# Last block: the convolution's taps over eight steps instead of seven, its norm, gates and output product one step later

## The chip, the cores and the metric

The kernel runs as one program on one of the eight cores of a Trainium2 chip. The metric is the device time of one launch in microseconds (us). Three runs of the kernel before gave a median of 1036.96 us (1036.89 to 1037.16). The profile shown here is one further execution that took 1037.11 us. A core has a matrix engine (PE, TensorE, with its weight loads listed apart as PEld), a vector engine (DVE), an activation engine (ACT), a general engine (POOL) and a queue that issues DMAs (SP). Each works through its own list of instructions in order, and they wait for each other by semaphores.

## The reference, cut to what matters

The program computes a chain of blocks on 256 tokens of 1024 channels: a gated linear attention with a feed-forward net, an attention with a feed-forward net, and then the last block, in which alone the change lies. Its input `h` goes through one wide matrix, whose columns are cut into parts:

```python
c_val, c_gate, c_og, ts, r_og, g_conv, g_rwkv = jnp.split(p, SPLITS, axis=-1)   # p = h @ w_in
u = c_val * sigmoid(c_gate)
u = causal_depthwise_conv(u, conv_k) + conv_b         # 31 taps for each of 1024 channels
u = layernorm(u, ln_g, ln_b)                          # over the channels
y_conv = (silu(u) * silu(c_og)) @ w_conv_out
y_rwkv = rwkv7_branch(ts, r_og) @ w_rwkv_out          # 16 heads of 64, a recurrence over the tokens
m = sigmoid(g_conv) * y_conv + sigmoid(g_rwkv) * y_rwkv
x = x + gate * (m @ w_out)                            # then a last rmsnorm
```

The two branches depend on `h` alone and meet in `m`.

## The kernel before

Activations lie transposed, channels on the 128 partitions and tokens along the free axis; 1024 channels are eight tiles of 128 x 256. Every product with a weight matrix is cut into dense blocks of 256 output columns. For a block, SP loads 1 MB of weights into one of three `raw` buffers; ACT copies it into a rounded high part (line 296, two halves), DVE subtracts to get the low part (line 304, two halves), and PE sums three products for each of eight input tiles and two output halves: high by high, high by low, low by high (lines 318 to 320), 48 matmuls in all. The blocks use the buffers in turn, so the split of block n + 3 waits until block n is done.

The last block has 48 dense blocks: r, k, v (inputs of the recurrence), val and gate (the convolution's input), og (the convolution's output gate), rog (the recurrence's), gr and gc (the two sigmoid gates of `m`), cout (the product with `w_conv_out`), rout (with `w_rwkv_out`) and out (with `w_out`), four of each. The recurrence works on pairs of heads, eight in all, as a software pipeline of steps s = -2 to 8 (loops over s and r at lines 1358 of PE, 1970 of ACT and 2748 of DVE). In step s, `chain` runs the recurrence over four chunks of tokens for pair s, `middle` prepares pair s + 1 (scores, then an inverse of a triangular matrix built up in five levels that go PE, DVE, PE, ACT and round again), `front` prepares pair s + 2, and `gn` normalises pair s - 1. A step has 12 slots (r = 0 to 11); each slot has two half slots (q = 0 to 23). These parts leave short stretches on every engine, and a table `STEP_BLOCKS` puts dense blocks between them: `put_blocks` cuts each block into eight units of six matmuls and deals them evenly over the 24 half slots of the step, together with the halves of the split of the block two further on ("hi" for ACT, "lo" for DVE), the evacuation from PSUM by ACT ("take", at the block's last unit) and what DVE does with it ("use", one half slot later). The order of `STEP_BLOCKS` is also the order of the loads on SP. All of this is fixed when the program is written: there is no scheduler.

The convolution is 248 instructions of DVE (31 taps for eight tiles, line 2614, the first of a tile line 2610), dealt over half slots by `TAP_SLOTS`: 164 half slots, from q = 4 of step -1 to the end of step 5. Three pairs of tiles are summed (`three_pairs`) when their taps are done. Then comes its layer norm, `ln`, in step 6: PE sums over channels (line 1087), DVE subtracts the mean (line 2632, eight tiles), ACT squares (line 1849), DVE folds (lines 2637, 2638), PE sums (line 1092), ACT takes the logarithm and the exponential (lines 1431, 1432), DVE scales (line 2643, eight tiles), ACT applies silu (line 1858, eight tiles). Each og block is evacuated by ACT into a gate tile (line 1817), DVE multiplies (line 2586), ACT rounds the product (`conv_y_hi`, line 1872) and DVE takes the low part (line 2656). These four pieces are the input of the cout blocks, whose units wait for them one by one (semaphore `conv_y_split`).

Before, og0 to og3 stand in step 6 behind the norm, and step 7 has gc3 first and then cout0 to cout3. In step 8, which has no recurrence left but the normalisation of the last pair, the first two rout blocks run tile by tile (`rout_part`) in banks 4 and 5 as the tiles of the recurrence's output come. The rest of rout and out stands behind the loop. The line numbers below are those of the kernel before; PE's small matmuls named there are line 1225 (first product of a chunk in `chain`), 1246 (`u_product`, which needs ACT's copy of line 1958), 1148 (scores), 1171 (`seeds`, which needs three results of DVE's `middle` at r = 0), 1195 and 1198 (the inverse's steps).

Of the kernel before, what the change touches and what calls it, by code (L numbers as in the profile page):

```python
# [184 lines left out]
def program(nc, a, out):  # L185
    with ExitStack() as ctx:
# [389 lines left out]
        for q, item in enumerate((("hi", N_ROUT + 2, 0), ("hi", N_ROUT + 2, 1), ("lo", N_ROUT + 2, 0),  # L576
                                  ("lo", N_ROUT + 2, 1))):
            put_at(8, 1 + q, item)
        for g in range(14):
            put_at(8, 12 * g // 14, ("rout_part", g // 7, g % 7))  # L580
# [13 lines left out]
        def _(pe):  # L594
# [455 lines left out]
            def unit(n, u):  # L1050
# [9 lines left out]
                if u == 7:  # L1060
                    last.then_inc(block_done, 1)

            def rout_part(j, k):

                n = N_ROUT + j
                if k == 0:
                    pe.wait_ge(w_lo_ready, n + 1)
                    bank_freed(n)
                pe.wait_ge(sem("rwkv_split"), k + 1)
                for m in range(2):  # L1070
                    ps, wh, wl, xh, xl = operands(n, m, k)
# [1798 lines left out]
```

## Time and profile before

| what | value |
|---|---|
| median of three runs | 1036.96 us |
| the profiled execution | 1037.11 us, its span 1035.3 us |
| PE busy, share of the span | 1006.3 us, 97% |
| PEld busy | 930.6 us, 90% |
| DVE busy | 869.3 us, 84% |
| ACT busy | 608.7 us, 59% |
| granted clock of PE in the steps of the last block | 1.00 |

The last block takes the part of the span from about 603 us on. A step is read best by PE's own marks: the matmuls of `u_product` at r = 1 (line 1246) of steps 0 to 7 start at 681.96, 720.18, 758.82, 798.53, 836.45, 870.28, 902.82 and 947.30 us, so that the distance of two of them is one step, from slot 1 to slot 1. A busy share in these stretches counts instructions that run; the waits are a view of their own, and where a matmul waits it is PEld that stands, since the weight load comes first.

### The profile page before, as it was taken

What the parts mean: (1) busy time and instruction counts of PE and PEld (TensorE: products, weight loads), DVE (VectorE), ACT (ScalarE), POOL (GpSimd) and SP (SyncE); (2) the same over time, 40 slices, a digit from 0 to 9 for tenths busy, and PEclk for the clock granted to TensorE, in tenths of its full rate; (3) what the DMA queues carried; (4) which work ended last, traced back from release to release, by engine and by line L of the source; (5) the groups of instructions that cost most, each with busy time, mean ns of one, the idle gap of its engine ahead of it and who ended that gap; (6) DMA issues with size and microseconds to landing.
All of it is one profiled execution on the core that took longest, in us unless ns stands there. A gap on an engine that the chain in (4) does not pass through costs nothing.

```text
span 1035.3 us, 23881 instructions
## 1 busy us (share of the span) xinstructions
PE 1006.3 (97%) x10130; PEld 930.6 (90%) x10130; DVE 869.3 (84%) x1447; ACT 608.7 (59%) x878; POOL 18.3 (2%) x38
## 2 busy tenths in 40 slices
PE   7999999999999999999999999999999999999997
PEld 6999999999999989989898998889998988889996
DVE  7866699899989886999899897998998999965474
ACT  7755664444446756554444577656667667686443
POOL 2000000000000000000000000000000000000000
PEclk9999999999999999999999999999999999999998
DMA  9662457777654515576765646333323322234531
GB/s 279 217 200 93 156 186 251 233 243 226 200 174 151 164 45 183 200 231 226 250 224 184 203 132 195 115 93 122 125 90 117 121 87 83 84 124 152 175 123 41
DMA packets 136071, 168.20 MB, mean 162 GB/s; under 512 B 3216, under 2 KB 125328, under 8 KB 135728
## 3 DMA queue, kind: packets, MB, share of 16 engines
q1 hardware_dynamic: 132080, 153.44, 46.0%
q0 software_dynamic: 3904, 13.50, 4.1%
q8 instruction: 66, 1.08, 0.4%
q14 instruction: 21, 0.17, 0.0%
HBM read 164.83 MB, written 2.10 MB: 161 GB/s over the span
## 4 chain that ended last, share of the span: by engine, by line
PE 73%; DVE 18%; ACT 5%; issue 2%; DMA 2%; SPq 0%; DVEq 0%; ACTq 0%
PE banks L353 13%; PE banks L318 9%; PE banks L319 8%; PE banks L320 8%; PE banks L355 7%; DVE hf L2614 3%; DVE w_parts L280 3%; DVE w_parts L304 2%; PE banks L655 2%; PE bank L657 2%; PE bank L655 2%; PE bank L659 2%; PE banks L657 2%; PE banks L659 2%; ACT w_parts L275 1%
## 5 line engine op out<-in xcount | busy, mean ns | idle before, releaser
L280 DVE TENSOR_TENSOR w_parts<-raw,w_parts 128x2048 fp32r<-128x2048 f32 x95 | 217.1, 2288 | 27.2 <-ACT w_parts L275 26.8
L353 PE MATMUL banks<-x_parts,w_parts 128*128 128x512 f32 x640 | 227.1, 399 | 0.0
L318 PE MATMUL banks<-x_parts,w_parts 128*128 128x256 f32 x704 | 211.7, 301 | 0.0
L319 PE MATMUL banks<-x_parts,w_parts 128*128 128x256 f32 x736 | 207.8, 282 | 0.0
L320 PE MATMUL banks<-x_parts,w_parts 128*128 128x256 f32 x704 | 198.7, 282 | 0.0
L275 ACT ACTIVATE w_parts<-raw 128x2048 fp32r<-128x2048 f32 x95 | 180.9, 1905 | 3.6 <-PE banks L810 2.1
L355 PE MATMUL banks<-x_parts,w_parts 128*128 128x256 f32 x640 | 179.8, 281 | 0.0
L353 PEld LDWEIGHTS banks<-x_parts,w_parts 128*128 128x128 f32 x640 | 120.3, 188 | 29.0
L318 PEld LDWEIGHTS banks<-x_parts,w_parts 128*128 128x128 f32 x704 | 134.0, 190 | 9.5 <-issue 3.3
L319 PEld LDWEIGHTS banks<-x_parts,w_parts 128*128 128x128 f32 x736 | 140.7, 191 | 0.6 <-issue 0.5
L320 PEld LDWEIGHTS banks<-x_parts,w_parts 128*128 128x128 f32 x704 | 134.3, 191 | 0.0
L355 PEld LDWEIGHTS banks<-x_parts,w_parts 128*128 128x128 f32 x640 | 121.0, 189 | 0.0
L304 DVE TENSOR_TENSOR w_parts<-raw,w_parts 128x1024 fp32r<-128x1024 f32 x86 | 103.7, 1218 | 15.9 <-ACT w_parts L296 15.8
L2614 DVE SCALAR_TENSOR_TENSOR hf<-big,vecs,hf 128x256 f32<-128x256 f32 x240 | 101.5, 479 | 0.0
L296 ACT ACTIVATE w_parts<-raw 128x1024 fp32r<-128x1024 f32 x86 | 87.5, 1058 | 11.1 <-PE banks L320 5.4
L1499 ACT ACTIVATE u<-banks 128x512 f32<-128x512 f32 x40 | 23.9, 598 | 81.8 <-PE banks L355 81.8
L2117 DVE SCALAR_TENSOR_TENSOR big<-u,vecs,big 128x256 f32<-128x256 f32 x168 | 70.0, 479 | 0.0
L1487 ACT ACTIVATE big<-big 128x512 f32<-128x512 f32 x20 | 12.6, 632 | 93.8 <-DVE big L2117 93.8
L655 PE MATMUL banks<-g_parts,w_parts 128*128 128x256 f32 x176 | 50.0, 284 | 1.4 <-DVE g_parts L2195 1.1
L655 PE MATMUL bank<-g_parts,w_parts 128*128 128x256 f32 x176 | 49.8, 283 | 0.0
L657 PE MATMUL bank<-g_parts,w_parts 128*128 128x256 f32 x176 | 49.8, 283 | 0.0
L659 PE MATMUL bank<-g_parts,w_parts 128*128 128x256 f32 x176 | 49.8, 283 | 0.0
(418 smaller groups left out, 2373.5 us busy)
## 6 DMA issues: line engine op xcount, KB each, us to landing
raw<-in_ffn_w_up SPq DMA_DIRECT2D x44, 1024.0 KB, 5.1
raw<-in_w_in SPq DMA_DIRECT2D x36, 1024.0 KB, 5.5
raw<-in_ffn_w_down SPq DMA_DIRECT2D x22, 1024.0 KB, 5.3
big<-in_ada_w_t POOLq DMA_DIRECT2D x24, 512.0 KB, 4.1
raw<-in_gla_w_in SPq DMA_DIRECT2D x11, 1024.0 KB, 5.6
raw<-in_attn_w_qkv SPq DMA_DIRECT2D x6, 1024.0 KB, 4.9
raw<-in_gla_w_out SPq DMA_DIRECT2D x4, 1024.0 KB, 4.9
raw<-in_attn_w_out SPq DMA_DIRECT2D x4, 1024.0 KB, 4.9
```

Of the source, the lines that this page charges most:

```text
L275: nc.scalar.activation(WH[:, n % RING, :, :], RAW[:, n % RING, :, :], ACT.Copy)\
L280: eng.tensor_tensor(WL[:, n % RING, :, :], RAW[:, n % RING, :, :], WH[:, n % RING, :, :].bitcast(F32), ALU.subtract).then_inc(w_lo_ready, 1)
L304: ins = nc.vector.tensor_tensor(WL[:, n % RING, ks, :], RAW[:, n % RING, ks, :], WH[:, n % RING, ks, :].bitcast(F32), ALU.subtract)
L318: nc.tensor.matmul(ps, wh, xh, start=start, stop=False)
L319: nc.tensor.matmul(ps, wh, xl, start=False, stop=False)
L320: return nc.tensor.matmul(ps, wl, xh, start=False, stop=stop)
L353: nc.tensor.matmul(PS[bank + m].rearrange("p (a t) -> p a t", a=2), WH[:, s, k, ms], XP[:, :, k, :], start=k == 0, stop=False, skip_group_ ...
L355: last = nc.tensor.matmul(PS[bank + m][:, 0:T], WL[:, s, k, ms], XH[:, k, :], start=False, stop=k == KT - 1, skip_group_check=True)
L655: nc.tensor.matmul(ps, wh[:, k, ms], GH[:, gk, :], start=start, stop=False, skip_group_check=True)
L657: nc.tensor.matmul(ps, wh[:, k, ms], GL[:, gk, :], start=False, stop=False, skip_group_check=True)
L659: ins = nc.tensor.matmul(ps, wl[:, k, ms], GH[:, gk, :], start=False, stop=stop, skip_group_check=True)
L2614: ins = v.scalar_tensor_tensor(CONV[:, k, :], U31[:, k, j:j + T], vec("conv_k_2", KT * j + k), CONV[:, k, :], ALU.mult, ALU.add)
```

## The change

The taps are dealt over one more step (188 half slots instead of 164), the norm, the og blocks and the rounding of the convolution's output go from step 6 to step 7, the cout blocks from step 7 to step 8. All four rout blocks stand whole behind the loop, in the two banks of the other blocks; `rout_part` goes. Steps 0 to 3 have three dense blocks instead of four, step 4 has four instead of three, step 5 three instead of two, step 6 three instead of five; step 7 has five as before, but gc3 and og0 to og3. Behind the loop the splits of rout2 to out3 on ACT and DVE are put into a new order. PE runs the same matmuls; ACT has two table loads more, DVE one subtraction less (seven tiles of the recurrence's output at once instead of six and one).

```diff
-    0: _blocks("gate1 val2 rog0 gate2"),
-    1: _blocks("r2 k2 v2 val3"),
-    2: _blocks("gate3 rog1 gr0 gr1"),
-    3: _blocks("r3 k3 v3 gr2"),
-    4: _blocks("rog2 gr3 gc0"),
-    5: _blocks("gc1 gc2"),
-    6: _blocks("rog3 og0 og1 og2 og3"),
-    7: _blocks("gc3 cout0 cout1 cout2 cout3"),
-    8: _blocks("rout0 rout1 rout2 rout3 out0 out1 out2 out3"),
+    0: _blocks("gate1 val2 rog0"),
+    1: _blocks("r2 k2 v2"),
+    2: _blocks("gate2 rog1 val3"),
+    3: _blocks("r3 k3 v3"),
+    4: _blocks("gate3 rog2 gr0 gc0"),
+    5: _blocks("gc1 gc2 gr1"),
+    6: _blocks("rog3 gr2 gr3"),
+    7: _blocks("gc3 og0 og1 og2 og3"),
+    8: _blocks("cout0 cout1 cout2 cout3 rout0 rout1 rout2 rout3 out0 out1 out2 out3"),
...
+        put_blocks(8, STEP_BLOCKS[8][:4])
-        for j, (s, q) in enumerate(((6, 11), (6, 15), (6, 20), (7, 0))):
+        for j, (s, q) in enumerate(((7, 11), (7, 15), (7, 20), (8, 0))):
...
-            put_at(6, q, ("ln", k))
-        TAP_FIRST, TAP_SLOTS = 4, 20 + 6 * 24
+            put_at(7, q, ("ln", k))
+        TAP_FIRST, TAP_SLOTS = 4, 20 + 7 * 24
...
-        put(4, 10, ("three_pairs",))
+        put(5, 9, ("three_pairs",))
...
-            for j in range(2):
-                rout_part(j, KT - 1)
-            whole(N_ROUT + 2)
-            whole(N_ROUT + 3)
+            for j in range(4):
+                whole(N_ROUT + j)
```

DVE at the end of step 1 and the start of step 2, before: the last block of step 1 is val3, which DVE does not touch. Line 2707 and the two rows behind it are `gn`, line 2723 opens `middle` of step 2.

```order
L304 TENSOR_TENSOR w_parts<-raw,w_parts 128x1024 [waits w_hi_ready]
L2614 SCALAR_TENSOR_TENSOR hf<-big,vecs,hf 128x256 [waits dve_steps] x3
L304 TENSOR_TENSOR w_parts<-raw,w_parts 128x1024
L2614 SCALAR_TENSOR_TENSOR hf<-big,vecs,hf 128x256 [waits dve_steps] x3
L2707 SCALAR_TENSOR_TENSOR big<-big,vecs,w_r 128x256 [waits gn_rstd]
L2709 SCALAR_TENSOR_TENSOR big<-big,vecs 128x256 [waits dve_steps]
L2712 TENSOR_TENSOR big<-big,pair_tiles 128x256 [waits evacuated,dve_steps]
L2723 TENSOR_TENSOR pair_tiles<-banks,consts 128x512 [waits scores_b,rwkv_out_summed]
```

The same place now (line 302 is 304 of before, 2589 is 2614, 2682 is 2707, 2698 is 2723); v2 is now the last block of the step.

```order
L302 TENSOR_TENSOR w_parts<-raw,w_parts 128x1024 [waits w_hi_ready]
L2589 SCALAR_TENSOR_TENSOR hf<-big,vecs,hf 128x256 [waits dve_steps] x3
L302 TENSOR_TENSOR w_parts<-raw,w_parts 128x1024
L2549 SCALAR_TENSOR_TENSOR big<-u,vecs,big 128x256 [waits evacuated]
L2549 SCALAR_TENSOR_TENSOR big<-u,vecs,big 128x256
L2589 SCALAR_TENSOR_TENSOR hf<-big,vecs,hf 128x256 [waits dve_steps] x2
L2682 SCALAR_TENSOR_TENSOR big<-big,vecs,w_r 128x256 [waits gn_rstd]
L2684 SCALAR_TENSOR_TENSOR big<-big,vecs 128x256 [waits dve_steps]
L2687 TENSOR_TENSOR big<-big,pair_tiles 128x256 [waits evacuated,dve_steps]
L2698 TENSOR_TENSOR pair_tiles<-banks,consts 128x512 [waits scores_b,rwkv_out_summed]
```

The two multiply-adds of v2 (line 2549), which wait for ACT's evacuation of the block that PE ends the step with, now stand ahead of the last taps, of `gn` and of `middle`. Step 3 ends with v3 in the same way.

ACT from the norm's root to the recurrence's third chunk, before, in step 6. Line 1961 and 1958 are the copies of `chain`, 1949 one of `middle`, 1817 the evacuation of og0, 1858 the silu, 1872 the first rounding.

```order
L1431 ACTIVATE ln_rstd_tile<-banks,consts 128x256 [waits ln_sums]
L1432 ACTIVATE ln_rstd_tile<-ln_rstd_tile 128x256 [waits act_steps]
L1961 ACTIVATE big<-banks 128x64 [waits u_summed]
L1817 ACT_TABLE_LOAD [waits gate_applied]
L1817 ACTIVATE gate_tiles<-banks 128x512 [waits block_done]
L296 ACTIVATE w_parts<-raw 128x1024 [waits block_done,raw_landed0]
L1858 ACTIVATE hf<-hf,vecs 128x256 [waits conv_normed]
L1858 ACTIVATE hf<-hf,vecs 128x256 x7
L1949 ACTIVATE big<-banks 128x512 [waits x_summed]
L296 ACTIVATE w_parts<-raw 128x1024
L1872 ACTIVATE conv_y_parts<-hf 128x512 [waits conv_y]
L1958 ACTIVATE att<-banks 128x64 [waits rhs_summed]
```

Now, in step 7 (1405 is 1431, 1935 is 1961, 1791 is 1817, 294 is 296, 1832 is 1858, 1846 is 1872, 1932 is 1958):

```order
L1405 ACTIVATE ln_rstd_tile<-banks,consts 128x256 [waits ln_sums]
L1406 ACTIVATE ln_rstd_tile<-ln_rstd_tile 128x256 [waits act_steps]
L1935 ACTIVATE big<-banks 128x64 [waits u_summed]
L1791 ACT_TABLE_LOAD [waits gate_applied]
L1791 ACTIVATE gate_tiles<-banks 128x512 [waits block_done]
L294 ACTIVATE w_parts<-raw 128x1024 [waits block_done,raw_landed1]
L1832 ACTIVATE hf<-hf,vecs 128x256 [waits conv_normed]
L1832 ACTIVATE hf<-hf,vecs 128x256 x7
L294 ACTIVATE w_parts<-raw 128x1024
L1846 ACTIVATE conv_y_parts<-hf 128x512 [waits conv_y]
L1932 ACTIVATE att<-banks 128x64 [waits rhs_summed]
```

The order is the same but for the copies of `middle`, which step 7 no longer has. What moved is the whole group, into a step in which PE has fewer small matmuls between the norm's parts.

ACT around the evacuation of og3, before, at the end of step 6 and the start of step 7; the two rows of line 296 are the split of cout1, line 1844 evacuates gc3.

```order
L1817 ACT_TABLE_LOAD [waits gate_applied]
L1817 ACTIVATE gate_tiles<-banks 128x512 [waits block_done]
L1958 ACTIVATE att<-banks 128x64 [waits rhs_summed]
L296 ACTIVATE w_parts<-raw 128x1024 [waits block_done,raw_landed0]
L296 ACTIVATE w_parts<-raw 128x1024
L1872 ACTIVATE conv_y_parts<-hf 128x512 [waits conv_y]
L1877 ACTIVATE rwkv_y_hi<-big 128x256 [waits rwkv_y]
L1961 ACTIVATE big<-banks 128x64 [waits u_summed]
L1844 ACT_TABLE_LOAD [waits v_turned,bonus_kept]
L1844 ACTIVATE big<-banks 128x512 [waits block_done]
```

Now, at the end of step 7 and the start of step 8:

```order
L1791 ACT_TABLE_LOAD [waits gate_applied]
L1791 ACTIVATE gate_tiles<-banks 128x512 [waits block_done]
L294 ACTIVATE w_parts<-raw 128x1024 [waits block_done,raw_landed1]
L294 ACTIVATE w_parts<-raw 128x1024
L1846 ACTIVATE conv_y_parts<-hf 128x512 [waits conv_y]
L1898 ACTIVATE w_r<-big 128x256 [waits rwkv_y,o_taken]
L1851 ACTIVATE rwkv_y_hi<-big 128x256 [waits rwkv_y]
```

The two halves of a split still stand between og3's evacuation and the last rounding (line 1846, before 1872). On PE, og3 was followed by gc3 and then cout0; now cout0 follows og3 at once, and its seventh tile waits for that last piece.

## Rows read from the trace of the kernel before

**Rows 1.** Windows: start:end, us, PE, PEld, DVE, ACT, POOL busy (x), clock, DMA.
```profile
720.20:758.80 38.60, 38.53 (x651) 34.97 (x650) 36.33 (x77) 25.29 (x50) 0.00 (x0) 1.00 0.34 107
836.50:870.30 33.80, 33.39 (x607) 29.59 (x606) 32.74 (x71) 24.59 (x44) 0.00 (x0) 1.00 0.28 86
870.30:902.80 32.50, 29.87 (x567) 25.73 (x566) 32.15 (x73) 20.84 (x38) 0.00 (x0) 1.00 0.29 90
1003.90:1026.90 23.00, 23.00 (x194) 23.00 (x193) 12.75 (x20) 11.10 (x20) 0.00 (x0) 1.00 0.04 15
```

**Rows 2.** Waits of PEld in step -1 (644.0 to 682.0): us, times, longest.
```profile
PEld banks L1198 <- DVE big L2735: 1.0, 1, 1.0
```

**Rows 3.** Waits of PEld in step 2 (758.8 to 798.5).
```profile
PEld banks L1148 <- issue: 0.9, 1, 0.9
```

**Rows 4.** Waits of PEld in step 5 (870.3 to 902.8).
```profile
PEld banks L1225 <- DVE att L2744: 1.5, 2, 1.1
PEld banks L1198 <- DVE big L2735: 1.1, 1, 1.1
```

**Rows 5.** Waits of PEld in step 6 (902.8 to 947.3).
```profile
PEld banks L1195 <- DVE big L2735: 1.2, 1, 1.2
PEld banks L1092 <- DVE big L2638: 0.8, 1, 0.8
```

**Rows 6.** Waits of PEld from cout's end to rout's (979.4 to 1003.9).
```profile
PEld banks L1072 <- DVE x_parts L2597: 1.0, 1, 1.0
```

**Rows 7.** Timeline, DVE, end of step 1: start, us, instruction, tiles, count.
```profile
753.40 1.22 DVE L304 TENSOR_TENSOR w_parts<-raw,w_parts 128x1024 fp32r<-128x1024 f32 x1
754.54 1.27 DVE L2614 SCALAR_TENSOR_TENSOR hf<-big,vecs,hf 128x256 f32<-128x256 f32 x3
755.72 0.48 DVE L2707 SCALAR_TENSOR_TENSOR big<-big,vecs,w_r 128x256 f32<-128x256 f32 x1
...
758.63 1.27 DVE L2614 SCALAR_TENSOR_TENSOR hf<-big,vecs,hf 128x256 f32<-128x256 f32 x3
```

**Rows 8.** Timeline, ACT and DVE, evacuation and use of block r2.
```profile
726.45 0.60 ACT L1823 ACTIVATE u<-banks 128x512 f32<-128x512 f32 x1 [3.98 <-PE banks L320]
...
727.80 0.88 DVE L2574 SCALAR_TENSOR_TENSOR big<-u,vecs,big 128x256 f32<-128x256 f32 x2 [0.24 <-ACT big L1825]
```

**Rows 9.** Timeline, PE, step 4: first small matmul and first of seeds.
```profile
832.29 0.27 PE L1225 MATMUL banks<-pair_tiles 64*64 64x64 f32 x2
...
837.22 0.27 PE L1171 MATMUL banks<-big,consts 64*64 64x64 f32 x2
```

**Rows 10.** Timeline, PE, step 6: the norm's two sums.
```profile
901.87 0.38 PE L1087 MATMUL banks<-u,consts 128*128 128x256 f32 x1
...
910.32 1.13 PE L1092 MATMUL banks<-big,consts 128*128 128x256 f32 x4 [0.55 <-DVE big L2638]
```

**Rows 11.** Timeline, ACT, step 6: table load, logarithm, end of silu, rounding.
```profile
913.95 1.28 ACT L1427 ACT_TABLE_LOAD   x1
915.24 0.47 ACT L1431 ACTIVATE ln_rstd_tile<-banks,consts 128x256 f32<-128x256 f32 x1
...
920.71 2.09 ACT L1858 ACTIVATE hf<-hf,vecs 128x256 f32<-128x256 f32 x5
...
924.13 0.62 ACT L1872 ACTIVATE conv_y_parts<-hf 128x512 fp32r<-128x512 f32 x1
```

**Rows 12.** Timeline, PE, step 7: slots 0, 1, 3 and 7 begin.
```profile
943.97 0.27 PE L1225 MATMUL banks<-pair_tiles 64*64 64x64 f32 x2
...
947.30 0.33 PE L1246 MATMUL banks<-att,big 64*64 64x64 f32 x4
...
952.74 0.27 PE L1225 MATMUL banks<-pair_tiles 64*64 64x64 f32 x2
...
965.01 0.27 PE L1246 MATMUL banks<-att,big 64*64 64x64 f32 x2
```

**Rows 13.** Timeline, DVE, step 7: the convolution output's last low part.
```profile
947.88 0.69 DVE L2656 TENSOR_TENSOR conv_y_parts<-hf,conv_y_parts 128x512 fp32r<-128x512 f32 x1 [0.22 <-ACT conv_y_parts L1872]
```

More of the change, by code:

```diff
@@ L85, in bank_of @@
         return 1
-    if N_ROUT <= n < N_ROUT + 2:
-        return 4 + n - N_ROUT
     return n % RING if n < N_L3 else n % 2
@@ L575, in program @@
             put_blocks(s, STEP_BLOCKS[s])
[L576 to L580, printed above, removed]
-        for j, (s, q) in enumerate(((6, 11), (6, 15), (6, 20), (7, 0))):
+        put_blocks(8, STEP_BLOCKS[8][:4])
+        for j, (s, q) in enumerate(((7, 11), (7, 15), (7, 20), (8, 0))):
             put_at(s, q, ("conv_y_hi", j))
@@ L1058, in unit @@
                         pe.wait_ge(sem("conv_y_split"), k // 2 + 1)
+                    if n == N_ROUT and m == 0:
+                        pe.wait_ge(sem("rwkv_split"), k + 1)
                     last = three(*operands(n, m, k), k == 0, k == KT - 1)
                 if u == 7:
[L1061 to L1071, printed above, removed]
-                    nc.tensor.matmul(ps, wh, xh, start=k == 0 and m == 0, stop=False, skip_group_check=True)
-                    nc.tensor.matmul(ps, wh, xl, start=False, stop=False, skip_group_check=True)
-                    last = nc.tensor.matmul(ps, wl, xh, start=False, stop=k == KT - 1, skip_group_check=True)
-                if k == KT - 1:
                     last.then_inc(block_done, 1)
@@ L1084, in ln @@
                     pe.wait_ge(sem("conv_done"), 1)
-                    pe.wait_ge(sem("gn_rstd"), 5)
+                    pe.wait_ge(sem("gn_rstd"), 6)
                     for m in range(2):
@@ L1133, in gn @@
                     pe.wait_ge(sem("bonus_kept"), min(8, p + 4))
-                    if p >= 5:
+                    if p >= 6:
                         pe.wait_ge(sem("ln_rstd"), 1)
@@ L1992, in m_hi @@
                     .then_inc(sem("m_hi"), 1)
+            split_hi_whole(N_ROUT + 2)
             split_hi_whole(N_ROUT + 3)
             m_hi(0)
+            split_hi_whole(N_OUT)
             m_hi(1)
-            split_hi_whole(N_OUT)
             split_hi_whole(N_OUT + 1)
@@ L2761, in _ @@
                         gn(s - 1, r + 8 if s == 8 else r)
-                    if (s, r) == (7, 4):
+                    if (s, r) == (8, 2):
                         dve.wait_ge(block_done, N_COUT)
-                        rwkv_y_lo(0, 6)
-                    if (s, r) == (8, 1):
-                        rwkv_y_lo(6, 7)
+                        rwkv_y_lo(0, 7)
             rwkv_y_lo(7, 8)
@@ L2787, in m_lo @@
                     .then_inc(sem("m_split"), 1)
+            split_lo_whole(N_ROUT + 2)
             dve.wait_ge(sem("cout_used"), 4)
             mix(0)
-            mix(1)
             split_lo_whole(N_ROUT + 3)
             m_lo(0)
+            mix(1)
+            split_lo_whole(N_OUT)
             m_lo(1)
-            split_lo_whole(N_OUT)
             mix(2)
             split_lo_whole(N_OUT + 1)
+            m_lo(2)
             mix(3)
-            m_lo(2)
             m_lo(3)
```

5 lines of the change are left out of this document (removed).

## The prediction

> **What bounds the kernel now.** I read the windows by step first, then PEld's waits step by step, then the timelines of DVE, ACT and PE around the places that the change touches. The windows show that in the last block PE is nearly always occupied: step 1, with four dense blocks, takes 38.60 us with PE busy for 38.53, although DVE is busy for 36.33 of them as well [rows 1]. So two engines are loaded almost evenly, and PE is ahead by a little. The stretch behind the loop gives the price of a block: 194 matmuls in 23.00 us are 0.119 us each, 48 of them 5.7 us [rows 1]. A step with three blocks (step 4) takes 33.80 us, one with two (step 5) 32.50, although two blocks less than in step 1 should save 11.4 us and not 6.1: there DVE sets the pace, busy for 32.15 of 32.50 us [rows 1].
>
> The matmuls stay the same, so the change can only move PE's waits. The waits are few: 1.0 us in step -1 [rows 2], 0.9 in step 2 [rows 3], 1.5 and 1.1 in step 5 [rows 4], 1.2 and 0.8 in step 6, where the norm stands [rows 5], and 1.0 where rout waits for the recurrence's output [rows 6]. That is 7.5 us, the most that the redistribution can win, if it added no wait at all. Steps 0, 1, 3 and 7 have none that a row shows.
>
> **The change part by part.**
>
> *Step -1.* The taps there go from 30 to 26 (20 half slots at 248/188 instead of 248/164). A tap costs 0.39 us, from three taps that fill 754.54 to 755.72 [rows 7], so DVE is 1.6 us lighter ahead of the place where PE waited 1.0 us for it. I take -1.0; it can't be more and may be 0.
>
> *Steps 0 to 3.* PE loses a block: 38.6 - 5.7 = 32.9 us. DVE loses the two halves of a split, 1.14 us apart [rows 7], so 2.3, and 4.6 taps, 1.8: in step 1, the heaviest, 36.33 - 4.1 = 32.2 us. Steps 1 and 3 keep three r, k, v blocks whose use is DVE's, so DVE is at 32.2 of 32.9, or 98%, between step 4 (32.74 of 33.80, 97%) and step 5 (99%) [rows 1]. Step 4 leaves PE idle for 0.41 us (33.80 less 33.39) [rows 1], step 5 has waits of 2.6 [rows 4]. I take 0.5 for each of steps 1 and 3, near step 4, and 0.1 for each of 0 and 2, in which DVE has no r, k, v.
>
> Something else is added. Before, a block without work for DVE ended steps 1 and 3 (val3, gr2); now v2 and v3 end them, and DVE meets their wait ahead of the last two taps, `gn` and `middle`, on which PE's `seeds` of the next step wait. From the start of ACT's evacuation to DVE's use is 1.35 us [rows 8], the use 0.8, two taps 0.8, `gn` with `middle` 2.91 (755.72 to 758.63) [rows 7]: 5.9 us. I let the evacuation begin together with the next step's first small matmul, since both follow the block's last dense matmul. PE needs 4.93 us from there to `seeds` in a step of three blocks [rows 9], and one unit more, 0.7, in one of four. So PE waits 1.0 us behind step 1 and 0.3 behind step 3. Together steps 0 to 3 have 0.2 + 1.0 + 1.3 = 2.5 us of waits, less the 0.9 that was in step 2: +1.6. Below, no wait at all gives -0.9; above, both heavy steps behave like step 5 and the two handovers stay: 5.2 + 1.3 - 0.9 = +5.6.
>
> *Steps 4 and 5.* Step 4 gets a fourth block and fewer taps, so PE covers everything: 0. Step 5 gets a third block. Its DVE load is 32.15 + 2.3 - 1.8, and the two additions of `three_pairs` come to it from step 4, each about the 0.69 us of a like instruction [rows 13]: 34.0 us. PE goes from 29.9 (32.50 less 2.6) to 35.6, less about 1 because the first slot of step 6, which this stretch holds, has one to two units less. So PE is the longer one again, by a little. I take 0.5 us of waits in place of 2.6: -2.1, between -2.6 and 0.
>
> *Step 6.* With the norm gone, the mask on which PE waited 1.2 us is no longer behind the norm's scaling on DVE, and the wait of 0.8 us of the second sum moves to step 7. DVE gets taps there but no `front`. I take 0.2 in place of 2.0: -1.8, between -2.0 and 0.
>
> *Step 7.* This is the price. The norm is a chain over four engines, and it now has less beside it. Count from its first sum on PE. Before, the second sum started 910.32 - 901.87 = 8.45 us later [rows 10]. In step 7, PE needs 0.95 us for the first sum (the next small matmul is at 902.82, the mark of step 6) and, with five blocks but no `middle`, 5.44 us from slot 1 to slot 3 [rows 12], so it stands ready 6.4 us later and waits 2.0. With the 1.06 us of the second sum (1.13 as listed, its last part overlapped) slot 3 begins at 9.5 and slot 7 at 9.5 + 12.3 = 21.8 [rows 12]. ACT's order is the second point: the silu ended 922.80 - 901.87 = 20.9 us after the first sum, and a split's half and the first rounding end at 924.75, 22.9 us after [rows 11]; only then comes the copy of `chain` for which PE's slot 7 waits, 0.2 us long. That makes a wait of 1.3 us. ACT has one copy of `middle` of 0.6 us and DVE one mask less in this stretch than in step 6, which I take off in part: 2.3 us in all for step 7, the near end being 0.7 (only the second wait, shortened), the far one 4.0 (both, and a slot's delay for og1 behind them).
>
> The table loads in this chain take 1.28 us, and the logarithm starts 0.01 us behind the load [rows 11]; both loads lie inside the 20.9 us. The Trainium skill ("ScalarE: Activation LUTs", section "What ACT_TABLE_LOAD costs") adds a drain of about 1.38 us to each switch. By that rule the two switches make the chain 2.8 us longer, which speaks against this change, and the sum below would be 1040.3 us. The row shows no gap for such a drain, so the sum goes without it.
>
> *Step 8.* Before, gc3 stood between og3 and cout0. Now cout0 follows og3, and its seventh tile needs og3's piece: from the end of og3 (the small matmul at 943.97) [rows 12] to the end of the last low part (947.88 + 0.69) [rows 13] are 4.6 us, in which ACT's queue still holds both halves of a split. PE covers six tiles, 18 matmuls, 2.1 us: a wait of 2.5. What it replaces is the wait of 1.0 us for the recurrence's output [rows 6], since four blocks of cout now hide the last pair's normalisation: +1.5, from -0.4 (if the piece comes 1.9 us sooner) to +3.6 (if nothing covers it).
>
> *Behind the loop.* rout2 to out3 are split in a new order. A split may start when the block three before it is done, so two blocks, 11.4 us, cover it; it takes two halves on ACT, each within the 1.33 us between the silu's end and the rounding [rows 11], and 2.3 us on DVE, 5.0 us in all. Nothing is added; if that cover were gone, it would be those 5.0 us once.
>
> *Sum.* -1.0 + 1.6 + 0 - 2.1 - 1.8 + 2.3 + 1.5 = +0.5 us on an execution of 1037.11 us (span 1035.3): 1037.6. That execution lies 0.15 us above the median of 1036.96, so 1037.5 us as a median.
>
> **The rivals.**
>
> *The waits go and few come (faster).* For it: the 4.9 us taken from steps -1, 5 and 6 are waits that rows show, while all that I add is pieced together. If steps 0 to 3 lose their wait (-0.9), the norm costs only 0.7 and cout's piece -0.4, the sum is -5.5: 1031.5 us; halfway between that and mine is 1034.5. Against it: DVE is at 98% in two steps.
>
> *The handover at the ends of steps 1 and 3 (slower).* DVE arrives at the use of v2 and v3 behind its time, since it has no slack in these steps, and then PE's `seeds` stand as step 5's matmuls did. For it: the step of before with DVE at 99% lost 2.6 us, and there the last block had no use. It decides once DVE's load in a step exceeds PE's 32.9 us. Price +5.6 in place of +1.6: 1041.5 us. Against it: step 4.
>
> *PE has room that its busy share hides (much faster).* PEld is busy for 34.97 of 38.60 us in step 1 [rows 1], so 3.6 us a step would be free, 14.5 in steps 0 to 3; won in full beside my +0.5, 1023.0 us. The Trainium skill ("Perfetto Trace Analysis", section "Identifying the Most-Contended Engine") says to judge PE's headroom by the busy share of its weight loads and not of its matmuls. Against it: in step 1 the matmuls leave 0.07 us of 38.60 open [rows 1], and the free tenth of the weight loads lies in the many switches between dense and small matmuls, whose number stays.
>
> *The change does not do what it says.* If DVE's taps never held PE in steps 0 to 3, taking some out of them wins nothing there; that is in my sum already, and steps -1, 5 and 6 alone give gains: without a change in steps 0 to 3 the sum is -1.1, 1035.9 us. It is part of the forecast's own range.
>
> **How the numbers follow.** A run of this kernel can tell about 0.2%, 2.1 us, from no change: faster means below 1034.9, slower above 1039.0. My forecast has 0.45 (0.36 within, 0.04 below, 0.05 above); the faster rival 0.25 (0.21 below, 0.04 within), the slower one 0.27 (0.23 above, 0.04 within), room in PE 0.03 (below). Faster 0.28, same 0.44, slower 0.28. The ends of the terms add up to -6.2 and +13.2; they don't come together. 8 times in 10 I expect 1033.0 to 1041.5, which takes in most of the faster rival's way to 1031.5 and the slower one to its price; beyond lie 0.1 on each side. The forecast's own range is 1034.9 to 1039.6.
>
> **What would show it.** Right: PE's waits in steps -1, 5 and 6 fall below 0.6 us each; steps 0 to 3 last 33 to 34.5 us; a wait of about 1 us before `seeds` at the start of step 2; in step 7 a wait before the norm's second sum (2.0) and before `u_product` of slot 7 (about 1); at the seventh tile of cout0 a wait of 2 to 3 us for DVE's last low part; no wait at rout0. Wrong: a wait in steps 1 and 3 of more than 2 us each on DVE's mask or state; waits in step 7 that exceed 4 us; or a stretch behind the loop longer than 69 us for twelve blocks, which would put a wait where I see none.

## The result and the profile after

| | median | lowest to highest | executions |
|---|---|---|---|
| before, on the same chip | 1037.00 us | 1036.68 to 1037.47 | 7 |
| after | 1039.46 us | 1039.06 to 1041.09 | 7 |

The ratio is 1.0028, with a 95% interval of 1.0019 to 1.0037: the change makes the kernel slower by 2.5 us. The forecast was 1037.5 us, with 1033.0 to 1041.5 for 8 times in 10 and 1034.9 to 1039.6 for its own case; the measured time lies in both, near the upper end of the second. The profiled execution has a span of 1037.5 us, 2.2 more than before, with PE busy for 1008.2 us and DVE for 869.9.

The matmuls of `u_product` at r = 1 (now line 1222) start at 680.32, 713.30, 748.15, 782.66, 817.34, 856.76, 889.55 and 922.14 us in steps 0 to 7; step -1 begins at 643.88 (at 644.02 before). The table takes the step lengths before and after, and takes off the dense matmuls that moved, counted between these marks, at 0.119 us each.

| steps | length before | after | dense matmuls | their time | the rest | forecast |
|---|---|---|---|---|---|---|
| -1 | 37.94 | 36.44 | -6 | -0.7 | -0.8 | -1.0 |
| 0 to 3 | 154.48 | 137.03 | -180 | -21.4 | **+4.0** | +1.6 |
| 4 | 33.83 | 39.41 | +42 | +5.0 | +0.6 | 0 |
| 5 and 6 | 77.01 | 65.37 | -48 | -5.7 | -5.9 | -3.9 |
| 7 to the end | 88.05 | 115.33 | +192 | +22.8 | +4.5 | +3.8 |

The norm's first sum lies in the row of steps 5 and 6 both times. Its second sum, 1.06 us of PE, moved from that row to the last one; without it the waits of these two rows fell by some 4.9 and grew by some 3.4. The rest adds up to +2.4; step -1 begins 0.1 us earlier, and the span grew by 2.2.

These are the windows by step after, with the columns of [rows 1]: steps 1, 2, 3 and 6, and a stretch behind the loop.

```profile
713.30:748.20 34.90, 33.68 (x607) 29.81 (x606) 30.22 (x67) 23.37 (x49) 0.00 (x0) 1.00 0.30 96
748.20:782.70 34.50, 33.69 (x607) 29.71 (x606) 33.25 (x72) 23.94 (x44) 0.00 (x0) 1.00 0.31 100
782.70:817.40 34.70, 34.04 (x613) 30.28 (x613) 31.51 (x69) 23.95 (x48) 0.00 (x0) 1.00 0.28 91
...
889.60:922.10 32.50, 32.12 (x579) 29.06 (x578) 25.46 (x53) 21.23 (x36) 0.00 (x0) 1.00 0.39 121
...
1005.70:1028.80 23.10, 23.10 (x194) 23.10 (x194) 12.03 (x18) 11.10 (x20) 0.00 (x0) 1.00 0.01 2
```

Step 1 took 38.60 us with PE open for 0.07 [rows 1]; now it takes 34.90 with 1.22 open, although DVE is busy for only 30.22 of them, 87%. The stretch behind the loop runs as it did, 194 matmuls in 23.10 us. The waits after, in the order of the steps -1, 0, 1, 1, 2, 2, 3, 4, 5, 6, 7 and 8, say where that comes from. (The waits of 0.3 us named "issue", which most steps of both kernels have, are left out. Of the second row of step 1 PE's own wait is shown, since it names what was waited for. L1174 is a step of the inverse, L1147 `seeds`, L1070 the norm's second sum, L316 a dense matmul.)

```profile
PEld banks L1174 <- DVE big L2710: 0.7, 1, 0.7
...
PEld banks L1201 <- DVE att L2719: 0.6, 1, 0.6
...
PEld banks L1201 <- DVE att L2719: 0.7, 1, 0.7
...
PE bank L1136 <- ACT big L1871: 0.4, 1, 0.4
...
PEld banks L1147 <- issue: 0.6, 1, 0.6
...
PEld banks L1201 <- DVE att L2719: 0.4, 1, 0.4
...
PEld banks L1201 <- DVE att L2719: 0.8, 1, 0.8
...
PEld banks L1124 <- issue: 0.9, 1, 0.9
...
PEld banks L1174 <- DVE big L2710: 0.3, 1, 0.3
...
PEld banks L1147 <- issue: 0.4, 1, 0.4
...
PEld banks L1070 <- DVE big L2613: 1.9, 1, 1.9
...
PEld banks L316 <- DVE conv_y_parts L2631: 2.5, 1, 2.5
```

The 2.6 us of step 5 [rows 4] and the 2.0 of step 6 [rows 5] are down to 0.3 and 0.4. In their place stand 1.9 before the norm's second sum, 2.5 at cout0's seventh tile where 1.0 had been before rout [rows 6], and a wait of `rhs_values` (L1201) on the recurrence's state (DVE, L2719) in each of steps 0 to 3, where before had none. Each of these is small, but they come in four steps. What makes them is to be seen on DVE, around the 0.8 us of step 3, with the matmuls of PE that make the state's input first:

```profile
801.33 0.23 PE L1252 MATMUL banks<-big 64*64 64x64 f32 x2
...
800.54 1.22 DVE L302 TENSOR_TENSOR w_parts<-raw,w_parts 128x1024 fp32r<-128x1024 f32 x1
801.68 1.27 DVE L2589 SCALAR_TENSOR_TENSOR hf<-big,vecs,hf 128x256 f32<-128x256 f32 x3
802.87 0.41 DVE L2665 TENSOR_TENSOR big<-big 128x256 f32<-128x256 f32 x1
803.31 0.42 DVE L2666 SCALAR_TENSOR_TENSOR big<-big 128x256 f32<-128x256 f32 x1
803.66 0.27 DVE L2719 SCALAR_TENSOR_TENSOR att<-att,chunk_decay,banks 128x64 f32<-128x64 f32 x1
```

The state's input is there at 801.56, but a split's low half, three taps and the two instructions of `front` at r = 7 stand in DVE's queue ahead of the state, which is 0.27 us long and starts at 803.66; PE has its last dense matmul issued at 803.15 and gets its next small one at 803.99.

Two of the waits are for ACT. In step 1 `turned_keys` (L1136) waits for the second sigmoid of `front` (L1871), in front of which ACT's queue has two table loads: one for the silu of rog0, which now ends step 0 in place of gate2, and one back to the sigmoid. In step 4 `scores` (L1124) waits for ACT's copy of the inverse (L1926). ACT is busy without a pause there, behind a table load ahead of the root of `gn`:

```profile
847.47 1.28 ACT L1401 ACT_TABLE_LOAD   x1
...
852.08 0.38 ACT L1926 ACTIVATE big<-banks 128x256 f32<-128x256 f32 x1
```

Before, the same load stood in step 2, at 788.52 (now line 1401, then 1427):

```profile
788.52 1.28 ACT L1427 ACT_TABLE_LOAD   x1
```

So the 0.9 us of step 2 before [rows 3] are not gone; they went to step 4, together with that load.

The two sums of the norm on PE, and the restart at cout0, after (the number in brackets is the idle time before):

```profile
921.18 1.03 PE L1065 MATMUL banks<-u,consts 128*128 128x256 f32 x4
...
929.31 1.13 PE L1070 MATMUL banks<-big,consts 128*128 128x256 f32 x4 [1.66 <-DVE big L2613]
...
959.03 0.28 PE L318 MATMUL banks<-conv_y_parts,w_parts 128*128 128x256 f32 x1
961.57 0.39 PE L316 MATMUL banks<-conv_y_parts,w_parts 128*128 128x256 f32 x1 [2.26 <-DVE conv_y_parts L2631]
```

From the first sum to the second are 8.13 us, where they were 8.45 in step 6 [rows 10]: the chain over the engines is as long as it was, and PE has less to put beside it.

### The profile page after: what moved, and what is told of

Read it like the earlier page. It is cut to its first block, busy times and chain, and to the rows that moved or that the text cites. A ratio compares the mean times of both kernels' runs of the same rounds, so it can differ in the third digit from the quotient of the medians.

```text
span 1037.5 us, 23882 instructions
## 1 busy us (share of the span) xinstructions
PE 1008.2 (97%) x10130; PEld 931.8 (90%) x10130; DVE 869.9 (84%) x1446; ACT 612.3 (59%) x880; POOL 18.3 (2%) x38
## 4 chain that ended last, share of the span: by engine, by line
PE 67%; DVE 22%; ACT 7%; issue 2%; DMA 2%; SPq 0%; DVEq 0%; ACTq 0%
PE banks L351 13%; PE banks L316 8%; PE banks L317 7%; PE banks L318 7%; PE banks L353 7%; DVE hf L2589 4%; DVE w_parts L302 3%; DVE w_parts L278 3%; PE banks L649 2%; PE bank L651 2%; PE bank L649 2%; PE bank L653 2%; PE banks L651 2%; PE banks L653 2%; ACT w_parts L273 1%
## 5 line engine op out<-in xcount | busy, mean ns | idle before, releaser
L317 PE MATMUL banks<-x_parts,w_parts 128*128 128x256 f32 x768 | 216.8, 282 | 0.0
L316 PE MATMUL banks<-x_parts,w_parts 128*128 128x256 f32 x704 | 212.6, 302 | 0.0
L318 PE MATMUL banks<-x_parts,w_parts 128*128 128x256 f32 x704 | 198.6, 282 | 0.0
L353 PE MATMUL banks<-x_parts,w_parts 128*128 128x256 f32 x640 | 179.8, 281 | 0.0
L316 PEld LDWEIGHTS banks<-x_parts,w_parts 128*128 128x128 f32 x704 | 133.9, 190 | 10.2 <-issue 3.3
```

What stands on the lines that cost most here:

```text
L316: nc.tensor.matmul(ps, wh, xh, start=start, stop=False)
L317: nc.tensor.matmul(ps, wh, xl, start=False, stop=False)
L318: return nc.tensor.matmul(ps, wl, xh, start=False, stop=stop)
L353: last = nc.tensor.matmul(PS[bank + m][:, 0:T], WL[:, s, k, ms], XH[:, k, :], start=False, stop=k == KT - 1, skip_group_check=True)
```

## The experiments

The theory was that the whole loss is waits of PE: the change takes away two places where PE stood, and opens others, at the norm, at cout0 and in the steps that now have three blocks. The rival was that PE's own time grew, so that a wait taken away comes back elsewhere. All kernels but two start from the changed one.

**Rounding first.** At the start of step 8 the planner puts the rounding of og3's piece ahead of cout2's halves.

```
+for j, (s, q) in enumerate(((7, 11), (7, 15), (7, 20), (8, 0))): ...
 put_blocks(8, STEP_BLOCKS[8][:4])
-for j, (s, q) in enumerate(((7, 11), (7, 15), (7, 20), (8, 0))): ...
```

> The changed kernel, with the rounding of og3's piece (its high part on ACT, its low part on DVE) issued ahead of the weight split's halves for cout2 at the start of step 8, and nothing else moved. Theory (the 2.2 us that the span grew are waits of PE): the wait at cout0's seventh tile falls from 2.5 us to 0.5 to 0.9, and the time from 1039.5 to about 1037.7 us. Rival A (PE's own work grew, and waits only take the place of each other): the time stays within 0.5 us of 1039.5. Rival B (the halves that now come later hold the weights of cout2): the wait returns at cout2 or cout3 and the time is 1039 us or more.

Measured: 1040.32 us (1038.79 to 1040.66), ratio to before 1.003 (1.002 to 1.004). A miss: counted from the start of one matmul to the start of the next, the wait is 2.34 us in place of 2.54. DVE of this kernel, from the gate of og3 to the low part:

```profile
957.93 0.69 DVE L2561 TENSOR_TENSOR hf<-hf,gate_tiles 128x512 f32<-128x512 f32 x1 [1.97 <-ACT gate_tiles L1791]
958.77 0.49 DVE L2682 SCALAR_TENSOR_TENSOR big<-big,vecs,w_r 128x256 f32<-128x256 f32 x1
959.29 0.48 DVE L2684 SCALAR_TENSOR_TENSOR big<-big,vecs 128x256 f32<-128x256 f32 x1
959.81 0.42 DVE L2687 TENSOR_TENSOR big<-big,pair_tiles 128x256 f32<-128x256 f32 x1
960.15 0.68 DVE L2631 TENSOR_TENSOR conv_y_parts<-hf,conv_y_parts 128x512 fp32r<-128x512 f32 x1
```

ACT rounded the piece at 958.71, about 1 us earlier against the wait, but on DVE the normalisation of pair 6 (`gn`, three instructions) still stands ahead of the low part. I had named ACT's queue in the prediction and had not looked at DVE's, which was the last to be done.

**The second sum later.** On PE alone, the norm's second sum goes behind slot 3 of step 7.

```
-elif item[0] == "ln":
+elif item[0] == "ln" and item[1] != 3:
     ln(item[1])
+if (s, r) == (7, 3):
+    ln(3)
```

> The changed kernel, with the norm's second sum on PE behind the dense work of slot 3 of step 7 in place of slot 2 (some 3.1 us more of PE's own work in front of it); the other engines' orders are as they were. Theory (the wait of 1.9 us is uncovered latency of the norm's chain): that wait goes, the chain behind it is about 1.1 us later and nothing waits for it, 1037.6 us. Rival (what is later in the chain is late at cout0 too): the wait at cout0's seventh tile grows by up to 1.1 us, or one before og0's use appears, 1038.6 us or more.

Measured: 1039.03 us (1037.51 to 1039.82), ratio 1.0017 (1.0008 to 1.0026). The wait of 1.9 us is gone, and from the mark of step 7 to its slot 10 PE needs 28.36 us in place of 29.74, 1.4 less; 0.5 and 0.3 come back at the state and at `u_product`. The lowest execution is 1.5 us below the lowest of the changed kernel, but the median only 0.4, and the profiled one not shorter at all. The windows of that execution, from the wait at cout0 on (the third column from the right is PE's granted clock):

```profile
957.50:960.00 2.50, 0.30 (x3) 0.10 (x1) 2.18 (x6) 2.48 (x5) 0.00 (x0) 0.99 0.91 378
960.00:963.50 3.50, 3.43 (x16) 3.43 (x17) 3.50 (x4) 1.32 (x2) 0.00 (x0) 0.52 0.86 296
```

And those of the changed kernel's profiled execution at the same place:

```profile
959.10:961.50 2.40, 0.21 (x2) 0.01 (x1) 2.08 (x6) 2.38 (x5) 0.00 (x0) 1.00 0.91 381
961.50:965.00 3.50, 3.43 (x27) 3.38 (x28) 3.50 (x4) 1.83 (x4) 0.00 (x0) 1.00 0.90 306
```

After PE has stood for 2.5 us the granted clock is at 0.52, next to the lower level of 1.2 GHz, for 3.5 us in the one and at full speed in the other; PE gets 16 matmuls done in place of 27. That costs 1.4 us: from cout0's wait to the final sums are 71.67 us in the one and 70.23 in the other. It also splits the executions into two groups. Of the changed kernel four lie at 1039.06 to 1039.46 (mean clock 0.998 or 0.999) and three at 1040.67 to 1041.09 (0.996); of this one four at 1037.5 to 1038.3 and seven at 1039.0 to 1039.8; of the kernel with the rounding first two at 1038.8 and 1039.0 and seven at 1040.1 to 1040.7. A median of such a kernel says in part how often the clock fell, so the lower groups are compared as well.

**r, k and v spread.** No step holds three of these blocks, and none ends a step.

```
-0: "gate1 val2 rog0"  1: "r2 k2 v2"   2: "gate2 rog1 val3"  3: "r3 k3 v3"
+0: "r2 gate1 rog0"    1: "k2 v2 val2" 2: "r3 gate2 rog1"    3: "k3 v3 val3"
```

> The changed kernel, with the r, k, v blocks spread over steps 0 to 3 (r2 gate1 rog0; k2 v2 val2; r3 gate2 rog1; k3 v3 val3), so that none of them ends a step and no step holds three of them. Theory (waits in the three-block steps come from DVE's queue: the use of the step's last block ahead of seeds, and the state's hop behind front and taps): the waits before seeds in steps 2 and 4 (0.6 and 0.3 us) go and the state waits of 0.4 to 0.8 in steps 1 and 3 shrink, in all -0.8 to -1.5 us, 1038.3 us. Rival (these waits are the latency of one hop between PE and DVE, whatever DVE holds): within 0.4 us of 1039.5.

Measured: 1039.85 us (1039.38 to 1041.38), ratio 1.0033 (1.0023 to 1.0042). Steps 0 to 4 take 33.55, 34.81, 33.96, 35.63 and 38.98 us, in all 0.5 more than in the changed kernel. The waits before `seeds` in steps 2 and 4 (0.6 and 0.3) are gone, so these did come from the use of v2 and v3 at the end of a step. But steps 0 and 2 end with rog0, as in the changed kernel, and rog1, and what ACT does with these takes the gain: at the start of steps 1 and 3 `turned_keys` waits 0.6 us for `front`'s second sigmoid, where the changed kernel waits 0.4 and not at all. ACT at the end of step 2, and the wait:

```profile
777.96 1.28 ACT L1809 ACT_TABLE_LOAD   x1
...
780.91 1.28 ACT L1870 ACT_TABLE_LOAD   x1
...
PE bank L1136 <- ACT big L1871: 0.6, 1, 0.6
```

The waits on the state are 0.8, 0.7, 0.6 and 0.8 in steps 0 to 3 in place of 0.6, 0.7, 0.4 and 0.8. So these, the larger part, hang neither on the place nor on the kind of r, k and v.

**Half the taps**, on the changed kernel and on the one before. Each tap works on 128 of 256 tokens, which leaves out half of the convolution.

```
-v.scalar_tensor_tensor(CONV[:, k, :], U31[:, k, j:j + T], ...
+v.scalar_tensor_tensor(CONV[:, k, 0:T // 2], U31[:, k, j:j + T // 2], ...
```

> The changed kernel with the convolution's taps on 128 of the 256 tokens; the other half of the convolution is left out, the number of instructions and their order stay. DVE gets some 40 us lighter over steps -1 to 6. Theory (DVE's load makes PE's sub-microsecond waits in steps 0 to 5): they fall from some 5.5 us to below 2, while the norm's 1.9 and cout0's 2.5 stay, since these are latencies of chains: 1035.5 to 1036.5 us. Rival (those waits are hops between engines and PE's own time): 1039 us or more.

> The kernel before with the taps on 128 of the 256 tokens (the other half of the convolution is left out). Theory: the waits on DVE in steps -1, 2, 5 and 6 go, some 4.5 us, and the recurrence's wait of 1.0 stays: 1032.0 to 1033.0 us, below the 1034.2 of the changed kernel with the same taps, so that with DVE out of the way the change still costs its two waits of the norm and of cout0. Rival (the redistribution of the dense blocks is a gain in itself, which DVE hides): 1034.5 us or more.

Measured: 1034.15 us (1033.63 to 1035.78) for the changed kernel, 1032.38 (1031.95 to 1032.51) for the one before, ratios 0.9978 (0.9969 to 0.9987) and 0.9955 (0.994 to 0.997) to the whole kernel before. Both have the theory's sign, and the second its size; the first came out 1.35 us below the range that I had given it. Steps 0 to 3 of the changed kernel, its windows with half taps:

```profile
679.10:711.60 32.50, 32.43 (x603) 29.04 (x602) 26.05 (x64) 21.85 (x39) 0.00 (x0) 1.00 0.30 99
711.60:745.50 33.90, 33.39 (x603) 29.63 (x602) 26.26 (x64) 23.05 (x48) 0.00 (x0) 1.00 0.30 96
745.50:779.20 33.70, 33.35 (x603) 29.57 (x602) 29.93 (x75) 23.66 (x44) 0.00 (x0) 1.00 0.31 96
779.20:813.20 34.00, 33.89 (x610) 30.17 (x608) 27.11 (x67) 23.69 (x48) 0.00 (x0) 1.00 0.29 95
```

Each is 0.5 to 0.9 us shorter than after, with DVE 3 to 4 us lighter; the waits of the norm's second sum and of cout0, 1.94 and 2.54 from start to start, stay to the hundredth. In the kernel before, the same cut leaves steps 0 to 3 as long as they were (38.21, 38.64, 39.70 and 37.92): with four blocks DVE never held PE there. Its gain lies in steps -1, 4 and 5 (1.5, 0.6 and 2.5 us); the waits of steps 2 and 6, which I had going too, stayed. So 2.9 of the 4.0 us that steps 0 to 3 gave up are DVE's taps. The other 1.0 is in step 1, 33.97 us with half taps for 38.64 less 5.7: 0.7 of it are two waits for ACT that step 1 of before did not have, 0.3 at `turned_keys` and 0.4 at `scores`, and the rest stays open.

**The blocks moved alone**, with the taps over the steps of before.

```
-TAP_FIRST, TAP_SLOTS = 4, 20 + 7 * 24
+TAP_FIRST, TAP_SLOTS = 4, 20 + 6 * 24
```

> One part of the change alone: its blocks, its norm and its gates as in the changed kernel, but the taps spread as before over 164 half slots (up to the end of step 5), 36 a step in place of 32. Theory (DVE sets these waits, and halving the taps took 0.4 to 0.8 us from each step): DVE is 1.8 us heavier in each of steps 0 to 4, where PE has a block less, so these get 0.5 to 1.0 us longer each, while steps 5 and 6 lose 0.5 each: 1041 to 1043 us. Rival (the spreading of the taps is worth nothing): 1039 to 1040 us.

Measured: 1049.16 us (1048.34 to 1050.08), ratio 1.0121 (1.0105 to 1.0136). The sign is the theory's, the size is not: steps -1 to 3 get 0.8, 1.0, 1.1, 1.5 and 1.0 us longer, its upper end or above, and step 4 not at all, but steps 5 and 6, which I had getting shorter, get 0.8 and 1.5 longer; the wait for `seeds` in step 6 alone is 1.9. Besides, the clock fell here behind the norm's wait:

```profile
937.00:938.50 1.50, 1.49 (x21) 1.04 (x21) 0.00 (x0) 0.00 (x0) 0.00 (x0) 1.00 1.05 373
938.50:942.00 3.50, 3.50 (x21) 3.50 (x18) 1.23 (x1) 3.34 (x5) 0.00 (x0) 0.51 0.17 59
```

PE had stood for 1.94 us up to 937.01, and 1.5 us after it had gone on the clock fell for 3.5 us; the slots from the mark of step 7 to slot 4 took 13.17 us in place of 11.67. So cout0's wait is not the only one with that price.

**cout0 in another order.** The two tiles of og3's piece in the first half go behind six tiles of the second half; the line stands in a copy of `unit` for cout0 alone.

```
+u = (0, 1, 2, 4, 5, 6, 3, 7)[u]
```

> The changed kernel, with cout0's 48 matmuls on PE in another order: the tiles of og3's piece (the last two of the first half) come behind the first six of the second half, 18 matmuls or 2.2 us later; nothing else moved. Theory (what the change costs is uncovered latency at this one place, and the lower clock that follows the wait in about every second run): the wait falls from 2.5 us to 0.4 or less, the granted clock stays at its full level behind it, the runs no longer fall into two groups, and the time goes from 1039.5 to about 1037.1 us. Rival (the wait returns at the next block, since ACT and DVE hold cout2's weights behind this piece): 1038.5 us or more.

Measured: 1037.01 us (1036.46 to 1038.72), ratio 1.0004 (0.9995 to 1.0013), the lower group at 1036.5 to 1037.0, 2.5 us below the changed kernel's. No wait is left between 956 and 1000 us. One point of the theory fails: four of eleven executions still lie at 1038.1 to 1038.7 with a clock of 0.997.

**Taps late.** More taps in steps 5 and 6, where DVE no longer has `front`.

```
-TAP_FIRST, TAP_SLOTS = 4, 20 + 7 * 24
+TAP_FIRST, TAPS_IN = 4, (22, 26, 26, 26, 26, 36, 38, 48)
 (each step's number spread evenly over its half slots)
-put(5, 9, ("three_pairs",))
+put(6, 4, ("three_pairs",))
```

> The changed kernel, with the 248 taps put as 22, 26, 26, 26, 26, 36, 38 and 48 in steps -1 to 6 in place of 26 to 32 in each, and the additions of three_pairs at slot 4 of step 6 in place of slot 9 of step 5. Theory (DVE's load in the three-block steps makes PE's sub-microsecond waits, while steps 5 and 6, where DVE has no front left, have room: 29.2 of 32.8 and 25.5 of 32.5 us): the steps -1 to 3 get shorter by 0.2 to 0.4 us each, steps 4 to 6 longer by 0.5 in all: 1038.6 us. Rival (these waits are single hops between the engines): within 0.4 us of 1039.5.

Measured: 1039.04 us (1037.49 to 1039.75), ratio 1.0018 (1.0009 to 1.0027), the lower group 1.4 us below the changed kernel's. Steps -1 to 4 take 35.69, 32.45, 33.96, 34.38, 33.96 and 39.25 us, 3.2 less in all; steps 5 and 6 give 0.5 and 1.2 back in waits on the state. Steps -1, 0, 1 and 3 are as long as with half the taps, to 0.02 us, with every tap computed.

**Both waits covered.** cout0 in the new order, and the second sum behind two more dense units, in slot 3.

> The changed kernel with both long waits of PE covered: cout0's tiles in the order of e10_cout_order, and the norm's second sum behind two more dense units (1.4 us and the slot's small matmuls), in slot 3 of step 7. Theory (the lower clock follows a wait of PE of about 2 us or more, in a part of the executions, at either place): the 1.9 us fall to 0.3 or less, the two groups of times become one, within 0.8 us from end to end, at about 1035.4 us. Rival (what is left of the groups in e10 does not hang on the norm's wait): a third of the executions stays some 1.4 us above the others.

Measured: 1034.94 us (1034.29 to 1035.43), ratio 0.9981 (0.9972 to 0.999). The eleven executions are one group. PE now comes to the sum without a pause:

```profile
928.91 0.28 PE L318 MATMUL banks<-x_parts,w_parts 128*128 128x256 f32 x1
929.03 1.03 PE L1087 MATMUL banks<-big,consts 128*128 128x256 f32 x4
```

**And the taps late**, 23, 28, 28, 28, 29, 34, 34 and 44 in steps -1 to 6, with the additions of `three_pairs` at slot 4 of step 6.

> The kernel of e11_both_covered with the 248 taps put as 23, 28, 28, 28, 29, 34, 34 and 44 in steps -1 to 6. Theory (late taps freed the steps -1 to 4 of 2.5 us in e8, and cost steps 5 and 6 1.7, since they had too many there): -1.5 to -2.2 us more, 1033.5 us, below both kernels by 0.3%. Rival (the state's hop in steps 5 and 6 takes all of it back): 1035 us or more.

Measured: 1031.49 us (1031.09 to 1031.88), ratio to before 0.9949 (0.9935 to 0.9962): below both kernels, by more than I expected. Steps 1 and 6, step 7 and the twelve blocks behind it:

```profile
712.00:746.00 34.00, 33.50 (x604) 29.67 (x604) 28.28 (x62) 23.04 (x48) 0.00 (x0) 1.00 0.30 96
...
886.30:918.90 32.60, 32.47 (x581) 29.22 (x580) 30.99 (x67) 21.15 (x35) 0.00 (x0) 1.00 0.35 112
918.90:952.00 33.10, 33.10 (x333) 30.73 (x333) 23.84 (x37) 24.70 (x41) 0.00 (x0) 1.00 0.38 130
952.00:1021.50 69.50, 69.50 (x579) 69.37 (x579) 45.61 (x57) 33.41 (x48) 0.00 (x0) 1.00 0.41 137
```

In step 6 DVE went from 25.46 to 30.99 us of work, and the step is as long as it was; PE has nothing open any more from step 7 to the end of the twelve blocks.

**The kernel before, with uneven taps**: 22, 40, 40, 40, 40, 36 and 30 in steps -1 to 5.

> The kernel before with its 248 taps put as 22, 40, 40, 40, 40, 36 and 30 in steps -1 to 5 in place of 30 and 36 in each, nothing else moved. It asks whether the gain of e12_all needs the change, or only the uneven taps. Theory (PE is the longer one in steps 0 to 3, with 38.6 us against DVE's 36.3, and the waits of 1.0 in step -1 and 2.6 in step 5 are DVE's): these two steps get 0.7 and 1.5 us shorter, step 3 and its neighbours lose 0.5 in all, 1035.3 us; the rest of e12's gain belongs to the blocks moved. Rival (DVE at 37.9 of 38.6 us turns steps 0 to 3 into steps like 5): 1039 us or more.

Measured: 1035.74 us (1035.34 to 1036.18), ratio 0.9989 (0.998 to 0.9998). Its steps with 40 taps show why it gains no more; here are steps 1 and 3:

```profile
718.00:757.50 39.50, 39.28 (x655) 35.43 (x654) 37.78 (x81) 25.34 (x50) 0.00 (x0) 1.00 0.33 106
...
797.20:835.90 38.70, 38.48 (x645) 34.67 (x644) 35.63 (x77) 24.39 (x49) 0.00 (x0) 1.00 0.32 101
```

Steps -1 and 5 get 1.5 and 1.6 us shorter, steps 1 and 3 get 0.85 longer each and step 4 gets 0.4. So the moved blocks are not a loss as such: with their two long waits covered and the taps laid where DVE has room, they end 4.3 us below the kernel before with the one uneven table tried on it. The kernel before with its own waits at the norm and at rout covered was not run.

## Why the prediction was right or wrong

- *The picture.* That the change can only move waits of PE held. Every experiment that took one of the two long waits away won most of it back (2.5 in the new order of cout0, 1.4 of 1.9 with the sum later, and with both covered the stretch from step 7 to the end fell from 115.3 to 111.0, by 4.3), so the rival that PE's own time grew falls. The rival of room that the busy share hides falls as well: what PE does not do in steps 0 to 3 it does behind the loop, at 0.119 us a matmul.
- *Step -1*: -0.8 for -1.0, with 0.7 of the wait left. More was to be had: with 22 taps there the step loses another 0.75.
- *Steps 0 to 3*: this is the step of the prediction that failed, "Together steps 0 to 3 have 0.2 + 1.0 + 1.3 = 2.5 us of waits, less the 0.9 that was in step 2: +1.6". It measures +4.0, inside the bounds of -0.9 and +5.6. I took the waits from DVE's busy share over a step, and put DVE at 98% in step 1. It is busy for 87% there and PE waits all the same, since the state's hop finds three taps and a split's half in front of it; a block less in a step is less time for that queue to drain. These waits are 0.6, 0.7, 0.4 and 0.8 us, 2.4 in all. The handover at `seeds` that I had foreseen is there, 0.6 and 0.3 for my 1.0 and 0.3, and goes when v2 and v3 no longer end a step. What I had not looked at is ACT's queue at the same place: rog0 at the end of step 0 costs 0.4 to 0.5 at the start of step 1.
- *Step 4*: +0.6 for 0. The wait of 0.9 on `scores`, for the copy of the inverse that ACT makes at the end of the step, came here from step 2, and 0.5 on the state went; I had not looked at that queue.
- *Steps 5 and 6*: some -4.9 for -3.9, the waits down to 0.3 and 0.4 for my 0.5 and 0.2. The kernel before had two more waits in step 5 than I listed, 0.4 each before `seeds` (line 1171) and line 1129, and these went too. And the 11.4 us of two blocks that I set against 6.1 in step 5 are 10.0, since that stretch holds 108 dense matmuls where step 1 has 192.
- *Step 7*: the norm's second sum waits 1.9 us for 2.0. The second wait of 1.3, before slot 7, did not come with this change; a smaller one, 0.3, came at such a place, behind the silu, when the sum was put later. ACT's first table load behind that sum, after:

```profile
932.05 1.28 ACT L1401 ACT_TABLE_LOAD   x1
933.35 0.47 ACT L1405 ACTIVATE ln_rstd_tile<-banks,consts 128x256 f32<-128x256 f32 x1
```

  The logarithm follows the load after 0.02 us. The Trainium skill's rule of a further drain of about 1.38 us ("ScalarE: Activation LUTs", section "What ACT_TABLE_LOAD costs") is not borne out here. Nor could it have lengthened the chain as I reckoned: the 20.9 us were measured with both loads in them.
- *Step 8*: 2.5 us at cout0's seventh tile for 2.5, as worked out. I had not counted what it triggers: three of seven executions are in the upper group, 1.6 us longer on average.
- *Behind the loop*: nothing added, as forecast. The twelve blocks took 71.9 us, more than the 69 that I had named as a sign of being wrong; 2.4 of them are the wait at cout0, and the kernels without it still need 69.6.

That the time fell inside the forecast's own range is partly luck: errors of opposite sign, +2.4 in steps 0 to 3, +0.6 in step 4 and +0.2 in step -1 against -1.0 in steps 5 and 6 and -0.4 in steps 7 and 8, left the sum for the profiled execution 1.7 us too low.

## What to carry to other kernels

Between two engines that answer each other, read what stands in the second one's queue ahead of the answer, not its share of busy time: work taken from the first also takes away the cover of each hop. Do so for every engine at that place: a block whose evacuation needs another activation table puts loads of 1.28 us into ACT's queue. When filler work (here the taps) can lie anywhere, weigh it by each step's free time; even spreading was worth 3.4 us less than this. A chain over several engines that moves to a place with less work beside it pays the difference, and reordering independent tiles of the consumer, a small change on one engine, covers it more surely than hurrying the producer.

## What the runs showed of the hardware

A pause of PE of 1.94 us or of 2.3 to 2.5 us amid nearly full work was followed, in some executions and not in others of the same program, by a stretch at the lower level of the granted clock (0.51 and 0.52 of 2.4 GHz in the windows of 3.5 us above). Each fall cost 1.3 to 1.6 us, by the two profiles above and by the means of the groups. The fall came at the end of the pause in one profile and 1.5 us after it in another. With a pause of 2.3 to 2.5 us in the program, mostly with the other before it, 3 of 7, 7 of 9, 7 of 11, 4 of 9, 4 of 10 and 7 of 11 executions were in the upper group; with the 1.94 us alone 4 of 11; with neither, none of 16. The profiles agree with the groups: those of the kernels with the rounding first, the sum later, r, k and v spread and the taps late, all taken in the upper group, show the fall at cout0 (windows at 0.50 to 0.52), and those of the changed kernel, of half the taps and of cout0 in another order, taken in the lower group, show none. The kernel with the blocks moved alone has both pauses and 2 of 4 in an upper group, and its profile, from the lower one, shows a fall too, behind the norm's wait.

The kernel before, whose longest wait in these steps is 1.2 us [rows 5], shows no second group: of 80 executions beside the experiments 79 lie between 1036.37 and 1037.73 us, and the one at 1038.64 has a mean clock of 0.998. The Trainium skill ("TensorE: Matmul & The Clock Gate", section "What's actually happening") has a gate that sets the clock by how busy PE has lately been; the direction agrees. What decides in which executions the same pause lowers the clock no run here shows.
